# Paged latent attention of one decoding step: cache rows turned on VectorE in 32x32 blocks, scores as 32x32 tiles on TensorE

## The reference, cut to what matters

```python
def page_step(carry, pages):
    rows = cache[layer, pages]
    logits = einsum('bqhc,bkc->bqhk', qc, rows) * MLA_SCALE        # 288 numbers deep
    return update(carry, logits, rows[..., :MLA_KV_LORA])          # running max, sum of exp, p @ values (256 wide)
```

## Time and profile before

| | |
|---|---|
| median of 3 runs | 2532.64 us (2529.53 to 2537.63) |
| profiled execution | 2533.61 us, its span 2531.8 us |
| PE busy | 2287.7 us (90% of the span) |
| DVE busy | 1017.0 us (40%) |
| ACT busy | 547.2 us (22%) |
| paged stage, first fetch issued to last copy ended | 845.45 to 1161.28 us |
| granted clock of TensorE, mean | 0.925 |

### The profile page before, as it was taken

One profiled execution on the slowest core, in us unless ns is written; L12 is line 12 of the kernel. 1 busy time (PEld: TensorE's weight loads), 2 busy tenths in 40 slices (PEclk: granted clock), 3 DMA queues, 4 the chain that ended last, 5 costly groups with the idle time before them and its releaser, 6 DMA issues. The chain is left out here.

```text
span 2531.8 us, 36348 instructions
## 1 busy us (share of the span) xinstructions
PE 2287.7 (90%) x15400; PEld 2022.5 (80%) x15400; DVE 1017.0 (40%) x1455; ACT 547.2 (22%) x970; POOL 59.8 (2%) x97
## 2 busy tenths in 40 slices
PE   7999987939899799995899989767999999999997
PEld 6999966725577677774788889546999999999997
DVE  4212135563566455552122232564532432432423
ACT  3100004411333333330111121233210110110111
POOL 0000000000200011000000000000000000000000
PEclk8999959659899999996899999886999999999999
DMA  5113032030893577772411110220111111111111
GB/s 184 46 45 125 17 110 82 29 112 14 271 327 106 208 265 269 275 239 39 174 46 46 50 37 26 81 78 22 46 50 51 42 51 43 50 48 45 42 51 76
DMA packets 179005, 247.89 MB, mean 98 GB/s; under 512 B 23219, under 2 KB 164507, under 8 KB 173516
## 3 DMA queue, kind: packets, MB, share of 16 engines
q1 hardware_dynamic: 166992, 162.04, 20.7%
q0 software_dynamic: 5904, 83.95, 9.3%
q10 hardware_dynamic: 5996, 0.25, 0.2%
HBM read 220.35 MB, written 69.87 MB: 115 GB/s over the span
## 5 line engine op out<-in xcount | busy, mean ns | idle before, releaser
L2320 PE MATMUL ps<-xn_hi,mlp_w_hi 128*128 128x344 f32 x768 | 164.2, 322 | 7.0 <-DVE mlp_w_lo L2134 5.3
L2320 PE MATMUL ps<-mlp_xn_lo,mlp_w_hi 128*128 128x344 f32 x768 | 163.7, 321 | 0.0
L2320 PE MATMUL ps<-u_lo,mlp_w_hi 128*128 128x344 f32 x768 | 163.0, 320 | 0.0
L2320 PE MATMUL ps<-xn_hi,mlp_w_lo 128*128 128x344 f32 x768 | 162.9, 320 | 0.0
L2320 PE MATMUL ps<-u_hi,mlp_w_hi 128*128 128x344 f32 x768 | 162.9, 320 | 0.0
L2320 PE MATMUL ps<-u_hi,mlp_w_lo 128*128 128x344 f32 x768 | 162.1, 319 | 0.0
L1155 PE MATMUL ps<-mats,mla_rows 128*128 128x128 f32 x1024 | 129.7, 279 | 12.5 <-DMA mla_rows<-in_cache_mla,page_rows 12.1
L2320 PEld LDWEIGHTS ps<-xn_hi,mlp_w_hi 128*128 128x128 f32 x768 | 129.8, 190 | 8.5 <-DVE mlp_w_lo L2134 6.4
L1155 PEld LDWEIGHTS ps<-mats,mla_rows 128*128 128x128 f32 x1024 | 111.6, 142 | 25.8 <-DMA mla_rows<-in_cache_mla,page_rows 12.3
L2320 PE MATMUL ps<-xn_hi,win_hi 128*128 128x344 f32 x576 | 123.4, 323 | 7.7 <-DVE win_lo L2585 7.7
L2320 PEld LDWEIGHTS ps<-u_lo,mlp_w_hi 128*128 128x128 f32 x768 | 130.0, 189 | 0.0
(11 more groups left out here) (376 smaller groups left out, 4004.4 us busy)
## 6 DMA issues: line engine op xcount, KB each, us to landing
out_s_dsa_w<-in_cache_dsa_w SPq DMA_DIRECT2D x8, 4094.0 KB, 81.7
oaT<-in_w_up SPq DMA_DIRECT2D x32, 512.0 KB, 4.2
oaT<-in_w_down SPq DMA_DIRECT2D x32, 512.0 KB, 3.8
obT<-in_w_in SPq DMA_DIRECT2D x23, 512.0 KB, 3.7
gate_w<-in_w_in SPq DMA_DIRECT2D x16, 512.0 KB, 4.0
out_s_dsa_w<-in_cache_dsa_w SPq DMA_DIRECT2D x8, 1022.0 KB, 17.2
s_kv_tile<-in_cache_dsa_w SPq DMA_DIRECT2D x12, 512.0 KB, 5.5
x_scr<-qkvT SPq DMA_DIRECT2D x1, 4128.0 KB, 15.4
```

The costliest lines, as they stand in the source:

```text
L2320: last = nc.tensor.matmul(out[:, t, 0:TC], w, x[:, k, t * TC:(t + 1) * TC], start=first, stop=stop)
```

## The change

The rows are turned by VectorE, from SBUF to SBUF: three instructions for a unit, each over three of the nine 32-number pieces of a row (CB = 9, CG = 3). VectorE's transpose turns each 32x32 block by itself, so the numbers of a piece come onto 32 partitions, and rows of the four partition groups stay in their groups. Each score matmul is therefore 32 partitions deep and 32 weight columns wide, with 256 columns; eight lie in the array at a time (four row groups i, two column groups g). Even units use column groups 0 and 1 (PSUM partitions 0 to 63), odd units 2 and 3. `rt` has one buffer; the semaphores `turned[k]` and `used[k]` pass each third of it between VectorE and TensorE. The probabilities are turned by 8 transposes of 64 partitions. ScalarE now copies the turned probabilities and the values, and makes a copy of the unit's queries for every unit. On TensorE the loop stays; on VectorE and ScalarE all 32 units are written out. The queries' layout has 64 small copies on POOL, and the merge reads the maxima by four small copies where one was.

```diff
-                for h in range(H):
-                    for r in range(4):
-                        link(nc.gpsimd.tensor_copy(qsr[32 * r:32 * r + 32, :, r, h],
+                link(nc.gpsimd.memset(qq[:, CB - 1], 0.0))
+                for r in range(4):
+                    for m in range(4):
+                        for c in range(2):
+                            link(nc.gpsimd.tensor_copy(qq[SQ * r:SQ * r + SQ, 4 * c + m],
+                                                       qs[SQ * m:SQ * m + SQ, c]))
+                    for h in range(H):
+                        link(nc.gpsimd.tensor_copy(qq[SQ * r:SQ * r + SQ, CB - 1, :, h],
...
             def _(pe):
-                def unit(b, v, u, before):
-                    pe.wait_ge(landed[v], (b + 1) * 16)
-                    turn_rows(b, v, u, (0, 1))
-                    if before:
-                        turn_probs(*before)
-                    turn_rows(b, v, u, (2, 3))
-                    turn_rope(b, v, u)
-                    if before:
-                        value(*before)
-                    score(b, v, u)
+                def score(u, s):
+                    pe.wait_ge(q_set, u + 1)
+                    at_least(pe, probs, u - 1)
+                    for k in range(CG):
+                        pe.wait_ge(turned[k], u + 1)
+                        pe.sem_inc(pe_at[0], 1)
+                        for c in range(k * (CB // CG), (k + 1) * (CB // CG)):
+                            for g in range(JG):
+                                for i in range(4):
+                                    last = nc.tensor.matmul(
+                                        ps[32 * (JG * s + g):32 * (JG * s + g) + 32, i, 0:JN * SQ], q_now[SQ * i:SQ * i + SQ, s, c, :],
+                                        rt[SQ * i:SQ * i + SQ, c, JN * g:JN * g + JN, :].rearrange("p n t -> p (n t)"),
+                                        start=(c == 0), stop=(c == CB - 1), tile_position=(SQ * i, 32 * (JG * s + g)),
+                                        skip_group_check=True)
+                        last.then_inc(used[k], 1)
+                def turn_probs(u, s):
+                    pe.wait_ge(probs, u + 1)
...
+                def value(u, s, v):
+                    pe.wait_ge(p_copied, u + 1)
...
+                def unit(u, v):
+                    score(u, v % 2)
+                    turn_probs(u - 1, (v - 1) % 2)
+                    value(u - 1, (v - 1) % 2, (v - 1) % UPB)
...
             def _(act):
+                def copy_probs(u):
+                    act.wait_ge(p_turned, u + 1)
...
+                for u in range(NU):
+                    if u:
+                        copy_probs(u - 1)
+                    exp(u)
+                    if u + 2 < NU:
+                        query(u + 2)
+                    if u:
+                        copy_values(u - 1)
...
             def _(dve):
+                def turn(u, k):
+                    v, n = u % UPB, CB // CG
+                    if k == 0:
+                        dve.wait_ge(landed[v], (u // UPB + 1) * 16)
+                    at_least(dve, used[k], u)
+                    nc.vector.transpose(rt[:, k * n:(k + 1) * n],
+                                        rows[:, v, :, k * n * SQ:(k + 1) * n * SQ].rearrange("p n (c f) -> p c n f", c=n)
+                                        ).then_inc(turned[k], 1)
...
+                for u in range(NU):
+                    if u + 1 < NU:
+                        turn(u + 1, 0)
+                    row_max(u)
+                    if u + 1 < NU:
+                        for k in range(1, CG):
+                            turn(u + 1, k)
```

More of the change, by code:

```diff
@@ L59 @@
 RG = UNIT // 4
+SQ = 32
+JG = 2
+JN = UNIT // JG
+CB = ROW // SQ
+CG = 3
 PARTS = UPB * 4
@@ L1087, in stage_mla @@
         rows = sb(st, "mla_rows", [P, UPB, UNIT, ROW])
[L1088 to L1092, removed]
+        rt = sb(st, "mla_rt", [P, CB, UNIT, SQ])
+        pr = sb(st, "smla_pr", [P, JN, 4, SQ])
+        half = [slice(0, JG * 32), slice(JG * 32, P)]
+        pt = sb(st, "smla_pt", [P, 2, JN, JG * 32])
         acc = sb(st, "smla_acc", [P, 2, KL + 2])
         negm = sb(st, "smla_negm", [P, 2])
-        q_now = sb(st, "q_now", [P, 2, 32])
-        qr_now = sb(st, "qr_now", [P, 4, 32])
+        q_now = sb(st, "q_now", [P, 2, CB, 32])
         landed = [sem(f"pages_in{v}") for v in range(UPB)]
[L1098 to L1101, removed]
+        turned, used = ([sem(f"smla_{x}{k}") for k in range(CG)] for x in ("rt_turned", "rt_used"))
+        q_set = sem("q_set")
+        pe_at = [sem("smla_pe_at_scores"), sem("smla_pe_at_probs")]
+        maxed, probs, own = sem("smla_maxed"), sem("smla_probs"), sem("smla_own")
         p_turned, p_copied, valued, acced = (sem("smla_p_turned"), sem("smla_p_copied"), sem("smla_valued"),
@@ L1104, in stage_mla @@
         stored = [sem("part_out0"), sem("part_out1")]
[L1106 to L1116, removed]
         part_in, rnew_in = sem("part_in"), sem("rnew_in")
@@ L1149, in _ @@
             def _(pe):
[L1150 to L1173, removed]
-                        for g in range(4):
[L1175 to L1183, removed]
@@ new lines, in turn_probs @@
+                def turn_probs(u, s):
+                    pe.wait_ge(probs, u + 1)
+                    at_least(pe, p_copied, u - 1)
+                    pe.sem_inc(pe_at[1], 1)
+                    for n in range(JN):
+                        last = nc.tensor.transpose(ps[:, 4 + s, n * JG * 32:(n + 1) * JG * 32],
+                                                   pr[half[s], n].rearrange("p i t -> p (i t)"),
+                                                   mats[half[s], C_ID + JG * 32 * s:C_ID + JG * 32 * (s + 1)])
+                    last.then_inc(p_turned, 1)
@@ L1218, in _ @@
+                def unit(u, v):
+                    score(u, v % 2)
+                    turn_probs(u - 1, (v - 1) % 2)
+                    value(u - 1, (v - 1) % 2, (v - 1) % UPB)
+                score(0, 0)
+                for v in range(1, UPB):
+                    unit(v, v)
                 with pe.Fori(1, NB) as b:
                     for v in range(UPB):
-                        unit(b, v, b * UPB + v, (b, (v - 1) % UPB, b * UPB + (v - 1)))
-                turn_probs(NB - 1, UPB - 1, NU - 1)
@@ L1288, in _ @@
-                for v in range(UPB):
-                    unit(0, v, v, (0, v - 1, v - 1) if v else None)
-                with dve.Fori(1, NB) as b:
-                    for v in range(UPB):
-                        unit(b, v, b * UPB + v, (b, (v - 1) % UPB, b * UPB + (v - 1)))
-                copy_probs(NB - 1, UPB - 1, NU - 1)
-                copy_values(NB - 1, UPB - 1, NU - 1)
+                for s in range(2):
+                    nc.vector.memset(acc[half[1 - s], s, KL:KL + 2], 0.0)
+                for k in range(CG):
+                    turn(0, k)
@@ L1357, in _ @@
                 dve.wait_ge(part_in, 16 * NB)
-                link(nc.vector.tensor_copy(m[:, 0:PARTS], part[:, :, KL]))
+                for s in range(2):
+                    for to in range(2):
+                        n, k = 4 * s + JG * s, 4 * s + JG * to
+                        last = nc.vector.tensor_copy(sub(m[:, k:k + 1], [8, UPB // 2], [1, JG]),
+                                                     sub(part[:, n, KL:KL + 1], [8 * (KL + 2), UPB // 2], [KL + 2, JG]))
+                link(last)
                 link(nc.vector.tensor_reduce(stat[:, 0:1], m[:], AX_X, ALU.max))
```

109 lines of the change are left out of this document (41 added, 68 removed).

## The result

The changed kernel took 2506.62 us, the median of 4 runs (2497.87 to 2516.67), beside 2533.67 us before (4 runs, 2529.53 to 2537.63). The ratio is 0.9897, with a 95% interval of 0.9872 to 0.9921: faster by 27 us. The forecast was 2480 us, a gain of 53.

The account below looks back on a forecast made before the run. PE was taken to bound the paged stage: 3.94 + 0.9 + 0.85 + 1.75 + 0.1 = 7.54, taken as 7.6 us a unit. With head, tail and merge that gave 53.4 us saved, 2480 us; own range 2464 to 2502, wide range 2462 to 2600.

Parts of the forecast that it names:

- the part on the order between engines: DVE and PE: maximum ends at E+1.65, later transposes at E+3.45 and E+5.25; PE's next scores start at E+3.6, in time.
- the part on ScalarE: ScalarE's copies and exponential take 2.8 us a unit, hidden behind PE; only the 0.60 us probability copy is on the path.
- The part on DMA: Page fetches use 88% of the engines; pages land 0.7 us late, only moving the next maximum to E+7.8, where it stands anyway.
- The scores' term: PE's 144 score records, eight in flight, make 18 groups of 0.219 us: 3.94 us a unit.
- Turning the probabilities and the wait for them: On PE before the values: 8 transposes 0.9 us, then 0.85 us idle until ScalarE's copy is done.
- four tiles in flight: Rival: PE runs only four score tiles at once, 11.5 us a unit, 2601 us; chance 0.04.
- a transpose of two cycles a number: Rival: each DVE transpose takes 3.35 us, making 11.7 us a unit on DVE, 2607 us; chance 0.06.
- the clock's: Rival: PE's clock falls to 1.2 GHz in steady state, 14.0 us a unit, 2679 us; chance 0.11.
- A clock that falls in a few units: PE's clock falls only in a few units and the kernel is still faster; chance 0.01.
- the loose pack: Rival: packing costs 30% of PE's score pace, scores 5.6 us, a unit 9.3 us, 2533 us; chance 0.04.
- GpSimd's added copies: POOL's 32 added copies of 256 numbers, some 0.4 us each, 12.8 us, fit before the next work; costed at nothing.
- the likeliest case: The main forecast of 2480 us, own range 2464 to 2502 us, chance 0.75.

Follow-up runs that it names:

- The kernel written out: All 32 units written out on PE instead of four and a loop, against the changed kernel: 2540.4 us; with four store slots too, 2535.49 us.
- the one with few pages: Four store slots and PE's units written out, but only the first four units fetch whole pages: 2468.17 us; with PE's loop instead, 2467.26 us.
- with the values copied first: Changed kernel with two slots, but ScalarE copies the preceding unit's values before the exponential: 2495.44 us, ratio 0.9871.

## Why the prediction fell short

The mechanism held: PE's chain a unit fell, and the stage with it. The gain was half of what was forecast, for one step left out, pauses that no row of before showed, and one term too small.

**The step that failed** is the part on the order between engines. It placed the maximum's end at E+1.65, with E the end of the scores, and asked only whether transposes and scores would be in time. `row_max` waits for `stored` (L1254's wait) as well, and the part on ScalarE called its work "hidden behind PE" without its order: the copy of the values stands behind the exponential. The next store hangs on that copy. The part on DMA saw the pages come late by 0.7 us and held that this only moved the maximum; it also moved the exponential, the copy and the store, until one store stood behind a fetch. In the place of "all are in time" the runs show a loop through VectorE, ScalarE, SyncE's store and back: 30.0 us of waits for stores, 10.5 us in which PE waited for the transposes behind them, and 14.8 us of time.

**PE's pauses** are not in the forecast either. PE's program grew to 184 matmul records a unit, each with its weight load. On the first pass of its loop PE ran out of instructions, because they came through the DMA engines that the page fetches filled. Without the store's loop this left 7.3 us. The trace of before had no pause there to warn of it. The Trainium skill, "Runtime: NRT & Kernel Launch", section "Instruction fetch mechanics", calls the cost of crossing into a new block of instructions mostly hidden. The kernel written out disagrees here, by 44 us; the one with few pages agrees.

**The scores' term was too small**: 4.52 us where 3.94 stood. Eight in flight was right: undisturbed they take 4.04 us, 0.1 above the sum. The other 0.5 us is a pause that comes with each issue of an indirect fetch. Its length was in no row of before. With what the other terms gave back, a unit took 7.79 us and not 7.6, 5.7 us over 30 units. With the 22.1 us of disturbed units this would be 27.8 us late. The stage was 24.5 late. The last two units, without a fetch beside their scores, took some 0.5 us less each. The last values, forecast at half clock with 3.4 us as before, ran at full clock in 1.93 behind a wait of 0.69. The rest of head and tail was about 0.8 us shorter.

**The other terms.** Turning the probabilities and the wait for them were put at 0.9 + 0.85 = 1.75 us and took 1.40: the wait was 0.69, and the transposes 0.71. Values: 1.75 forecast, 1.86 measured. Together the two give back 0.24 of the 0.58 us that the scores took too long. DVE's transpose, worked out from copies as 1.76, took a mean of 1.755. The rivals of four tiles in flight and of a transpose of two cycles a number are refuted, and so is the clock's in the steady state. A clock that falls in a few units had been given 0.01; it did fall there, behind waits of 1.9 to 3.2 us, and cost 5.6 us. For the loose pack, eight tiles undisturbed lost 0.10 of 3.94 us. VectorE's wait for pages in steady state was up to 1.65 us, 1.1 on average, where 0.7 was forecast. It delayed the maximum by up to 0.55 us in some units, and PE not at all. GpSimd's added copies cost nothing: the stage began no later. What the merge and the later stages gave back was 2.6 us, not 0.5; no experiment split it.

The chances were honest about the sign, 0.76 for faster, and the time lies within the wide range. But the likeliest case's own range ended at 2502, and a wait left out made it too narrow.

## What to carry to other kernels

When one engine's unit gets shorter, walk around every ring of buffers that the unit uses, the output's too. A ring that had slack (two slots, 9.4 us a unit) may have none at 7.8 if a store can stand behind a page fetch, and a late step can then make the next one late for many units. Give an output slots enough that no compute engine waits for a store, and place the copy that frees or fills a ring ahead of work that may wait. If a program issues many small instructions while DMA is nearly full, keep it in a loop, and expect the loop's first pass and the units ahead of it to be slow.

## What the runs showed of the hardware

- TensorE stops when its instructions have to be fetched through DMA engines busy with page fetches: pauses of up to 4.70 us in the kernel written out, each ending 1.2 to 1.6 us after a 16 KB packet of instructions, 44 us in all, and none with the same fetching and hardly any pages. The loop of 4 units fetched none in its later passes (no packet of q8 between 980 and 1100 us).
- An indirect fetch issued by GpSimd comes with a pause of TensorE's weight loads of about 0.6 us that ends 1.3 us after the issue began. The plain DMA issues of 0.54 us had none. Whether the issue or the start of the page traffic does it stays open: the kernels with few pages took both away. It is not a stop of every weight load: before, four loads of 128x32 ran at 984.34, 0.80 us after the issue of 983.54, where the changed kernel's stand still from 0.7 to 1.3 us after it. The Trainium skill, "DMA: Bandwidth & Descriptors", section "Terms", says that descriptors of GpSimd's DMAs are written to rings in SBUF, from which PE also reads its weights; no run here shows that this is the cause.
- Eight 32x32 tiles of float32 run at once: 144 records of 256 columns in 4.04 us, 0.224 us a group of eight, where a group of four took 0.219 before. The pack loses 2%.
- VectorE turns 32x32 blocks of float32 at the pace of a plain copy: 1536 numbers a partition in 1.755 us.
- A store of 129 KB issued 0.2 us after a page fetch landed in 2.1 to 3.4 us before, and in 2.7 to 3.5 in the changed kernel. Issued 1.0 to 4.9 us after one, it landed with it, 9.3 to 10.7 us after the fetch's issue, in all eight cases. One exception, unexplained: with the values copied first, a store issued 0.2 us after the fetch took 8.1 us.
- TensorE's granted clock fell to 0.50 in the changed kernel behind idle stretches of 1.9 to 3.2 us, and in the kernel written out behind one of 4.13 us. It stayed at 1.00 in the steady state with an idle 0.69 us in every unit, while the last values before ran at half pace behind 0.78 us.
